# Second mixer: one folded query-key map in place of query and key products, and values evicted tile by tile in place

## What is computed

```python
xc = silu(dwconv(xm, w_conv, b_conv))      # xm: the projected input, 2048 channels
q = blockdiag(xc, w_q)                     # blocks of 4 x 4, 512 of them
k = blockdiag(xc, w_k)
v = blockdiag(xm, w_v)
g = concat([q, k, v]) @ w_gates + b_gates  # gates of the scan, both directions
# per head, in parallel form: scores = q k^T (scaled), weighted by exp of gate sums, times v
```

## Time and profile before

| | |
|---|---|
| median of 3 runs | 2737.75 us (2736.78 to 2738.44) |
| the profiled execution, its own time | 2737.4 us |
| its span in the trace | 2735.8 us |
| PE busy | 2497.5 us (91%) |
| DVE busy | 1879.6 us (69%) |
| ACT busy | 1316.4 us (48%) |
| POOL busy | 277.1 us (10%) |
| mean granted clock of PE | 0.951 |

### The profile page before, as it was taken

The page is one execution under the profiler, slowest core; times in us unless marked ns, Lnnn a source line. Parts: engine busy times, 40 slices in busy tenths (PEclk is TensorE's granted clock), DMA queues, the critical chain, the costliest instruction groups (busy, mean ns, idle before and its releaser), DMA issues.

```text
span 2735.8 us, 29938 instructions
## 1 busy us (share of the span) xinstructions
PE 2497.5 (91%) x10799; PEld 1780.6 (65%) x10799; DVE 1879.6 (69%) x2074; ACT 1316.4 (48%) x1262; POOL 277.1 (10%) x330
## 2 busy tenths in 40 slices
PE   6999889968999999999389988998896999999993
PEld 3555444537888888888178765554444888888883
DVE  2999944537888888887467322554245888888885
ACT  2000022116777777776232323454114777777773
POOL 0535402300000000000100020000000000000001
PEclk9999999978999999999699998999997999999997
DMA  9010447259999999997811321103429999999993
GB/s 325 31 62 31 159 156 261 108 238 364 379 389 384 385 380 392 380 391 297 323 62 62 110 107 58 66 27 107 176 76 356 384 389 380 385 393 385 381 381 115
DMA packets 150405, 672.85 MB, mean 246 GB/s; under 512 B 24714, under 2 KB 34186, under 8 KB 93890
## 3 DMA queue, kind: packets, MB, share of 16 engines
q1 hardware_dynamic: 127698, 592.72, 56.4%
q0 software_dynamic: 20208, 74.98, 7.4%
q10 hardware_dynamic: 2432, 4.26, 0.4%
HBM read 612.58 MB, written 59.33 MB: 246 GB/s over the span
## 4 chain that ended last, share of the span: by engine, by line
PE 86%; DMA 5%; DVE 3%; ACT 2%; issue 1%; POOL 1%; SPq 1%; POOLq 0%; DVEq 0%; ACTq 0%
PE ps L779 82%; ACT arena L1226 2%; PE ps L936 1%; PE ps L942 1%; DMA xs_d<-arena 1%; DMA buf_d<-arena,slots 1%; DMA chunk<-in_w_ada_dram 1%; DMA arena<-buf_d,slots 1%; PE ps L867 1%; DMA arena<-buf_d 1%; DMA arena<-in_w_out_c_dram 0%; SPq L383 0%; DMA buf_d<-arena 0%; POOL arena L660 0%; PE ps L1197 0%
## 5 line engine op out<-in xcount | busy, mean ns | idle before, releaser
L1753 DVE TENSOR_TENSOR wl<-wx,wh 128x2048 fp32r<-128x2048 f32 x432 | 969.3, 2286 | 45.8 <-ACT wh L1226 45.7
L1226 ACT ACTIVATE wh<-wx 128x2048 fp32r<-128x2048 f32 x432 | 819.7, 1916 | 151.9 <-PE ps L779 147.0
L779 PE MATMUL ps<-arena 128*128 128x512 f32 (+5 forms) x2436 | 822.4, 511 | 33.3 <-ACT arena L1226 20.1
L779 PE MATMUL ps<-wh,xT 128*128 128x512 f32 x2304 | 736.2, 396 | 4.9 <-DVE xT L1770 4.9
L779 PEld LDWEIGHTS ps<-arena 128*128 128x128 f32 (+1 forms) x2436 | 429.9, 192 | 397.1 <-issue 352.9
L779 PEld LDWEIGHTS ps<-wh,xT 128*128 128x128 f32 x2304 | 435.1, 189 | 105.8 <-DVE xT L1770 5.7
L779 PE MATMUL ps<-wl,xT 128*128 128x512 f32 x1152 | 455.2, 395 | 0.0
L1226 ACT ACTIVATE arena<-ps 128x512 f32<-128x512 f32 (+4 forms) x289 | 173.0, 627 | 558.2 <-PE ps L779 446.0
L779 PE MATMUL ps<-wh,gT 128*128 128x512 f32 x1152 | 377.9, 399 | 0.0
L779 PEld LDWEIGHTS ps<-wl,xT 128*128 128x128 f32 x1152 | 217.6, 189 | 47.3
L779 PEld LDWEIGHTS ps<-wh,gT 128*128 128x128 f32 x1152 | 216.8, 188 | 47.2
(11 more groups left out here) (233 smaller groups left out, 1986.8 us busy)
## 6 DMA issues: line engine op xcount, KB each, us to landing
wx<-in_w_dram SPq DMA_DIRECT2D x432, 1024.0 KB, 7.8
arena<-in_w_ada_dram SPq DMA_DIRECT2D x40, 1024.0 KB, 9.3
arena<-buf_d POOLq DMA_DIRECT2D x38, 512.0 KB, 9.9
buf_d<-arena POOLq DMA_DIRECT2D x36, 512.0 KB, 7.2
craw<-in_w_in_c_dram SPq DMA_DIRECT2D x8, 2048.0 KB, 8.1
buf_d<-arena POOLq DMA_DIRECT2D x1, 14848.0 KB, 51.7
arena<-in_w_in_ab_dram SPq DMA_DIRECT2D x8, 1024.0 KB, 13.0
arena<-in_w_out_ab_dram SPq DMA_DIRECT2D x4, 2048.0 KB, 8.5
```

The source lines that it names most:

```text
L779: return pe.matmul(bank_ap, lhsT, rhs, start=first, stop=last)
L1226: return act.activation(out_, in_, f, **kw)
L1753: v.tensor_tensor(wl[:, g], wx[:, g], whs[g % NH].bitcast(F32), ALU.subtract).then_inc(m["low"], 1)
```

## The change

With block-diagonal Q and K (x times Q, x times K), q k^T is xc Q K^T xc^T. The new kernel makes F = Q K^T once and multiplies only the latent tokens by it; the scores are then taken against `xc` itself. F needs Q^T and K^T on the stationary and moving side, so DVE transposes `BD[:, 1]` and `BD[:, 2]` in 32 x 32 blocks, which is the full transpose since the blocks off the diagonal are zero, into a new array `bqk`. PE makes 16 products of 128 columns (four "folds" of four), and ACT writes F over `BD[:, 0]`, which the values no longer need.

Values are evicted token tile by token tile: `V_BANKS` names seven banks that are used in turn over all 24 tiles, `v_mm` counts tiles, and a tile is written back to the places of `xm` that it was made from (`values(h, tt)`: four pieces of 128 columns). PE's wait for R_G moves from the first value product to the sixth tile, when bank 2 is first overwritten.

```diff
+        bqk = at(45168, 2 * KE, P)
+        def values(h, tt):
+            o = tt * P + (2 if tt < CT else 4)
+            return xm[:, h * HC:(h + 1) * HC, o:o + P]
...
# SP, u == 2
-                    sp.wait_ge(kq_mm, KE)
+                    sp.wait_ge(fq_mm, FOLDS + KE)
...
# POOL, masks of unit 0
-                if u:
+                if u == 0:
+                    pool.wait_ge(fq_mm, FOLDS)
+                else:
...
# PE, values
-                pe.wait_ge(gr, R_G) if h == 0 else pe.wait_ge(v_ev, 6 * h)
                 for tt in range(NT):
+                    n = NT * h + tt
+                    if n == len(V_BANKS) - 2:
+                        pe.wait_ge(gr, R_G)
+                    if n >= len(V_BANKS):
+                        pe.wait_ge(v_ev, n - len(V_BANKS) + 1)
...
-                        ins = mm(ps[:, tt, cc * P:(cc + 1) * P], xm[:, t, o:o + P], BD[:, 0, t, :], True, True)
-                ins.then_inc(v_mm, 1)
+                        ins = mm(ps[:, V_BANKS[n % len(V_BANKS)], cc * P:(cc + 1) * P], xm[:, t, o:o + P], BD[:, 0, t, :], True, True)
+                    ins.then_inc(v_mm, 1)
                 mods(28 + h)
+            pe.wait_ge(v_ev, NT * H)
+            for i in range(FOLDS):
+                pe.wait_ge(bt_rdy, len(ROUNDS) + FOLDS)
+                for t in range(4 * i, 4 * i + 4):
+                    ins = mm(ps[:, i, t % 4 * P:(t % 4 + 1) * P], bqk[:, KE + t, :], bqk[:, t, :], True, True)
+                ins.then_inc(fq_mm, 1)
...
# PE, keys and queries
-                b0 = 4 * (t % 2)
-                if t >= 2:
-                    pe.wait_ge(k_ev, 2 * (t - 1))
-                    pe.wait_ge(q_ev, t - 1)
-                pe.wait_ge(bd_rdy, len(ROUNDS) + KE + t + 1)
-                mm(ps[:, b0, 256:512], BD[:, 1, t, :], xc[:, t, 0:S_CTX], True, True)
-                mm(ps[:, b0 + 1, :], BD[:, 1, t, :], xc[:, t, S_CTX + 2:], True, True)
-                mm(ps[:, b0 + 2, :], BD[:, 2, t, :], xc[:, t, S_CTX + 2:], True, True).then_inc(kq_mm, 1)
-            pe.wait_ge(k_ev, 2 * KE)
+                pe.wait_ge(f_ev, max(t // 4 + 1, min(t - 1, FOLDS)))
+                if t >= len(Q_BANKS):
+                    pe.wait_ge(q_ev, t - len(Q_BANKS) + 1)
+                mm(ps[:, Q_BANKS[t % len(Q_BANKS)], :], BD[:, 0, t, :], xc[:, t, S_CTX + 2:], True, True).then_inc(fq_mm, 1)
             pe.wait_ge(q_ev, KE)
...
# PE, attention
-                    ins = mm(ps[:, 6, :], AT[:, s * P:(s + 1) * P], vv[h][:, s, :], s == 0, s == NT - 1)
+                    ins = mm(ps[:, 6, :].rearrange("p (c n) -> p c n", n=P), AT[:, s * P:(s + 1) * P], values(h, s), s == 0, s == NT - 1)
...
# ACT
+            def v_out(h):
+                for tt in range(NT):
+                    n = NT * h + tt
+                    act.wait_ge(v_mm, n + 1)
+                    go(values(h, tt), ps[:, V_BANKS[n % len(V_BANKS)], :].rearrange("p (c n) -> p c n", n=P), ACT.Copy).then_inc(v_ev, 1)
+            v_out(0)
             act.wait_ge(gr, R_F)
...
-            for h in range(3):
+            for h in range(1, H):
                 v_out(h)
             act.wait_ge(gr, R_X)
             go(r_fl[0:64, :], r_x[0:64, :], ACT.Exp, scale=-1.0).then_inc(ga, 1)
-            v_out(3)
             vector_out(7)
-            for t in range(KE):
-                act.wait_ge(kq_mm, t + 1)
-                b0 = 4 * (t % 2)
-                go(xc[:, t, 0:S_CTX], ps[:, b0, 256:512], ACT.Copy).then_inc(k_ev, 1)
-                go(xc[:, t, S_CTX + 2:], ps[:, b0 + 1, :], ACT.Copy).then_inc(k_ev, 1)
+            for i in range(FOLDS):
+                act.wait_ge(fq_mm, i + 1)
+                go(BD[:, 0, 4 * i:4 * i + 4, :].rearrange("p t n -> p (t n)"), ps[:, i, :], ACT.Copy).then_inc(f_ev, 1)
...
# DVE, after R_M
+            v.wait_ge(bd_rdy, len(ROUNDS) + 2 * KE)
+            for i in range(FOLDS):
+                v.transpose(bqk[:, 8 * i:8 * i + 8].rearrange("p t n -> p (t n)"),
+                            BD[:, 1 + i // 2, 8 * (i % 2):8 * (i % 2) + 8].rearrange("p t n -> p (t n)")).then_inc(bt_rdy, 1)
             v.wait_ge(stt_mm, 1)
...
-                v.wait_ge(kq_mm, t + 1)
-                v.tensor_copy(qT[:, t, :], ps[:, 4 * (t % 2) + 2, :]).then_inc(q_ev, 1)
+                v.wait_ge(fq_mm, FOLDS + t + 1)
+                v.tensor_copy(qT[:, t, :], ps[:, Q_BANKS[t % len(Q_BANKS)], :]).then_inc(q_ev, 1)
...
+V_BANKS = (0, 1, 7, 4, 5, 2, 3)
+Q_BANKS = (4, 5, 0, 1, 2, 3)
+FOLDS = 4
```

More of the change, by code:

```diff
@@ L220, in program @@
             "raw_in bd_rdy bt_rdy gp_rdy ge_mm ge_rdy g_mm gr ga ar_st stt_mm st_rdy")
-        v_mm, v_ev, kq_mm, k_ev, q_ev = sems("v_mm v_ev kq_mm k_ev q_ev")
+        v_mm, v_ev, fq_mm, f_ev, q_ev = sems("v_mm v_ev fq_mm f_ev q_ev")
         ab_in, hn_in = sems("ab_in hn_in")
@@ L332, in program @@
         qT = at(30832, KE, S_LAT)
-        vv = [at(A_XM + HC * XM * h, NT, DH) for h in range(H)]
+        bqk = at(45168, 2 * KE, P)
+        def values(h, tt):
+            o = tt * P + (2 if tt < CT else 4)
+            return xm[:, h * HC:(h + 1) * HC, o:o + P]
         Ef, Eb, A0, A1, AT = (at(45168 + S * i, S) for i in range(5))
@@ L1152, in _ @@
             ins.then_inc(stt_mm, 1)
-            pe.wait_ge(v_ev, 6 * H)
             pe.wait_ge(st_rdy, 2)
             for t in range(KE):
-                b0 = 4 * (t % 2)
-                if t >= 2:
-                    pe.wait_ge(k_ev, 2 * (t - 1))
-                    pe.wait_ge(q_ev, t - 1)
-                pe.wait_ge(bd_rdy, len(ROUNDS) + KE + t + 1)
-                mm(ps[:, b0, 256:512], BD[:, 1, t, :], xc[:, t, 0:S_CTX], True, True)
-                mm(ps[:, b0 + 1, :], BD[:, 1, t, :], xc[:, t, S_CTX + 2:], True, True)
-                mm(ps[:, b0 + 2, :], BD[:, 2, t, :], xc[:, t, S_CTX + 2:], True, True).then_inc(kq_mm, 1)
-            pe.wait_ge(k_ev, 2 * KE)
+                pe.wait_ge(f_ev, max(t // 4 + 1, min(t - 1, FOLDS)))
+                if t >= len(Q_BANKS):
+                    pe.wait_ge(q_ev, t - len(Q_BANKS) + 1)
+                mm(ps[:, Q_BANKS[t % len(Q_BANKS)], :], BD[:, 0, t, :], xc[:, t, S_CTX + 2:], True, True).then_inc(fq_mm, 1)
             pe.wait_ge(q_ev, KE)
```

## The result

The changed kernel takes 2702.72 us (median of 4 runs, 2700.41 to 2704.38) against 2737.27 us (median of 4 runs) before: ratio 0.9877, 95% interval 0.9865 to 0.9890, or 34.6 us. The forecast was 2705.4, range 2701.5 to 2711. The profiled execution took 2704.38 us with a span of 2702.8.

A forecast was written before the change was run, and what follows sets the result against it. Around the change the wait chain ran through the gate chain, PE and ACT alternating over values, then PE alone, with clock losses after pauses. First scores 32.2 us earlier took 2737.4 to 2705.2; forecast 2705.4, range 2701.5 to 2711.

The forecast's parts named there:

- the rival with the cheaper burst: Folds on PE: clock does not drop, folds take 3.75 us, time 2703.2, or 2702 with quicker transposes; chance 0.09.
- PE has no pause in the values: Value products on PE run unbroken at full clock for 27.1 us, from 1624.36 to 1651.5.
- Abs 1.2 us later, behind the sixth eviction: Gate chain on ACT: Abs begins at 1630.6 instead of 1629.39, making the whole chain 1.2 us later.
- Four transposes 4.75 us: DVE, end of gate chain: 1.19 us each, ending at 1654.6, while PE stands from 1651.5.
- Folds 5.9 us: PE behind the transposes: 16 products, 3.75 us at full clock plus 2.15 for the low clock after the pause.
- Statistics 1.6 us: PE behind the folds: eight transposes and the wait for DVE's copies take 1.6 us, to 1662.1.
- `exps(0)` and `abc` covered: Masks and exponentials ready at about 1664, some 18 us before `scores(0)` ends, so they delay nothing.
- Scores 32.2 us earlier: First score products move from 1709.25 to 1677.0: 23.2 us from key and query products, 9.0 from values.
- the dearer one: Between values and queries: transposes of 1.78 us each or a longer low clock; time 2707.7 to 2711, chance 0.13.
- The bank waits: Query products: PE waits for banks to be handed back, losing 20 us; time 2725.6, chance 0.02.
- the slow operand: Attention's value products: operand in pieces read at half rate, 84.5 us more, time 2790; chance 0.03.
- no effect: First scores hardly move because the gate chain or `abc` sets them; time within 0.2%, chance 0.01.

The follow-up runs named there:

- the second profile of the changed kernel: The changed kernel run again, same code, on one chip with the transposes-in-gap version; length 54.00 us, median 2702.48 us.
- the PSUM source alone: Changed kernel with DVE taking the forget rows from PSUM with the bias added, evictions still ahead of Abs; length 52.47 us, time 2701.28 us.
- the transposes in the gap: Changed kernel with DVE's four transposes moved to where DVE waits for ACT's Abs, Exp and Ln; length 47.56 us, median 2695.76 us, again 2695.77.
- one query bank: Changed kernel with one bank for the query products in place of six; length 77.87 us, time 2730.00 us.

## Why the prediction was right, point by point

All from the first selection product, forecast against the profiled execution of the changed kernel.

The mechanism held at every step but one, what holds DVE's copy (below), and that one did not set the time. How near the number came is in part luck. By the forecast the length is 54.2; it was 52.81 in the first profile and 54.00 in the second, and the lower clock behind the pause could have been anything from nothing to 2.9 us. The median of 2702.72 lies just below my own inner range (2702.8 to 2708), close to the 2703.2 of the rival with the cheaper burst, though in that profile the folds were not cheap. There is a slip in the last step as well: 2705.2 and 0.35 make 2705.55, not 2705.4.

- *PE has no pause in the values, done 28.7 us behind that point.* Right: 1651.47 - 1623.57 = 27.9. I had added the pieces without their small overlaps. (The 24 and 16 that I called products of `mods` are records, 12 and 8 products; the times stand.)
- *Abs 1.2 us later, behind the sixth eviction.* 0.9 later: 7.5 us behind that point against 6.6 before. In that execution DVE's copy, held by POOL, ended at the same moment as the eviction (1631.07, 1631.12). The eviction is what held Abs where the copy was earlier, as in the second profile of the changed kernel and with the PSUM source alone (7.45 in both). That POOL is behind 3.3 of the copy's 3.85 us I did not see.
- *Four transposes 4.75 us, done 31.8 behind.* 4.63, done 31.4 behind.
- *Folds 5.9 us.* 5.44 here. The mechanism is shown by the transposes in the gap (3.84 without the pause, and the same in all four executions without one). Its size is not a constant: over the executions with a pause of 2.2 to 5.6 us ahead of them the folds took 3.81, 5.21, 5.44 (twice), 5.47, 5.68 and 6.73 us.
- *Statistics 1.6 us.* Mis-sized: 1661.59 - 1660.57 = 1.0. I took the transposes of before, which ran at the low clock, for their price at the full one.
- *Queries 14.1 us, last copy 0.75.* 14.02 and 0.77.
- *`exps(0)` and `abc` covered.* Right: `exps(0)` ran at 1661.57, while the queries were made.
- *The value operand in pieces costs nothing.* 12.16 a unit in place of 12.14, 0.3 us in all.
- *Scores 32.2 us earlier.* 33.6. The difference is made of the statistics (0.6), the folds (0.5), and the transposes' end (0.4).

The rivals: the cheaper burst is not excluded but happens at times (3.81 with one query bank). Of the dearer one, the second profile of the changed kernel shows a part: folds of 6.73, but transposes of 1.2 and queries at full clock in 14.00. The bank waits are out by the changed kernel's own trace (16 query products in 14.02 us without a pause), the slow operand by its pitch of 12.16, and "no effect" by the result.

What stays open is why the same code met a pause of 3.54 us with 3.81 us of folds in one execution and 6.73 in another. The rows show that it depends on when the clock falls (within the pause, during the folds or not at all) and when it comes back; they do not show what sets these moments.

## What to carry to other kernels

When one part of a change shortens a stage and another adds work to a chain that runs beside it, work out where the two meet afterwards: here each part gave 18 us alone, both gave 33.6, and moving one step (the transposes) into a gap of another engine's chain gave 38.9. A new step on DVE that depends on old data belongs in the first gap after its data are ready, not where the code that uses it begins. Look first at what it will run beside: POOL's maps, moved later, cost 2.2 us. And ask of every duration that a sum takes over whether it is the operation's own: one that is four times that of operations of its size may be a wait in disguise.

## What the runs showed of the hardware

- A DVE copy of 64 x 768 floats took 0.56 us with POOL idle and 3.76 to 4.78 us beside a run of POOL operations; in ten profiles it ended 0.41 or 0.42 us after the last of them, and POOL was not slowed (11.47 to 11.50 us for 32). An operation with two SBUF inputs took 2.96 in place of 0.95 us for the same reason. A `tensor_scalar` from PSUM took 1.02 us with POOL at work.
- The same burst of 16 fp32 products took 3.81 to 6.73 us behind pauses of about 3.5 us, and 3.84 in all four executions without a pause. The granted clock went to 0.50 within the pause (6.73 and 5.21 us, back earlier in the second), 1.5 us into the burst (5.44) or not at all (3.81).
- PE that works 1.10 us and stands 0.87 us in turn fell from the full clock to the half one after five such rounds and stayed there.
- A moving fp32 operand in runs of 128 is read at nearly full rate (12.16 us a unit against 12.14), and one with a step of two floats costs 5% (0.045 us on a product of 0.88).
